# One masked product per head in a state-space chunk stage, with two products moved to GpSimd

## The reference

```
acs    = cumsum(dt * A)                      # in a chunk
Lmat   = exp(where(i >= j, acs[i] - acs[j], -inf))
y_diag = sum_j (C[i] . B[j]) * Lmat[i, j] * dt[j] * x[j]
y_off  = (C[i] . h_prev) * exp(acs[i])
y      = forward(y_diag + y_off) + backward(y_diag + y_off) + d_skip * x
y      = y * silu(z);  y = y * rsqrt(mean(y * y) + eps) * norm_g
```

## Time and profile before

| | |
|---|---|
| median of 3 runs | 1816.97 us (1810.83 to 1821.08) |
| span of the profiled execution | 1810.1 us (its own time, from the first to the last instruction; the page gives no other) |
| busy in the span | PE 1716.3 (95%), PEld 1410.0, DVE 900.0, ACT 596.6, POOL 402.3 us |
| the chunk stage in it | from about 852 to 1012 us |

### The profile page before, as it was taken

The page is one execution under the profiler, slowest core; times in us unless marked ns, Lnnn a source line. Parts: engine busy times, 40 slices in busy tenths (PEclk is TensorE's granted clock), DMA queues, the critical chain, the costliest instruction groups (busy, mean ns, idle before and its releaser), DMA issues. The chain is left out here.

```text
span 1810.1 us, 27115 instructions
## 1 busy us (share of the span) xinstructions
PE 1716.3 (95%) x10438; PEld 1410.0 (78%) x10439; DVE 900.0 (50%) x1031; ACT 596.6 (33%) x1011; POOL 402.3 (22%) x275
## 2 busy tenths in 40 slices
PE   7999999999999989999999999997999998997997
PEld 6878888877877767777888888786777777785786
DVE  5202777202134137742788424323767789951674
ACT  5211222231111136642455313212543443443232
POOL 1011111111211101002100022000255565652330
PEclk9999999999999989999899999999999999998999
DMA  6211222323456312017675334223856778743452
GB/s 214 79 59 60 79 78 79 120 75 108 131 180 192 109 55 65 27 67 223 203 203 150 123 134 163 68 88 117 307 210 243 269 275 306 287 172 138 132 196 93
DMA packets 115837, 265.91 MB, mean 147 GB/s; under 512 B 13011, under 2 KB 59555, under 8 KB 115740
## 3 DMA queue, kind: packets, MB, share of 16 engines
q1 hardware_dynamic: 99772, 209.76, 35.4%
q0 software_dynamic: 8320, 30.43, 5.0%
q10 hardware_dynamic: 7648, 24.35, 3.8%
HBM read 192.95 MB, written 71.55 MB: 146 GB/s over the span
## 5 line engine op out<-in xcount | busy, mean ns | idle before, releaser
L2187 DVE TENSOR_TENSOR ex_wlo<-ex_raw,ex_whi 128x1024 fp32r<-128x1024 f32 x102 | 152.9, 1501 | 8.5 <-ACT ex_whi L2181 5.2
L2183 DVE CAST ex_whi<-ex_raw 128x1024 fp32r<-128x1024 f32 x96 | 114.3, 1191 | 45.4 <-DMA ex_raw<-experts 40.7
L2765 PE MATMUL rt_p<-ex_whi,ex_xh 128*128 x280 | 114.5, 409 | 14.5 <-DVE ex_wlo L2187 8.6
L286 PE MATMUL rest_p<-hi_h,whi_in 128*128 128x512 f32 (+1 forms) x480 | 122.2, 363 | 0.0
L286 PE MATMUL rest_p<-lo_h,whi_in 128*128 128x512 f32 (+1 forms) x480 | 120.5, 359 | 0.0
L286 PE MATMUL rest_p<-hi_h,wlo_in 128*128 128x512 f32 (+1 forms) x480 | 120.1, 359 | 0.0
L2766 PE MATMUL rt_p<-ex_wlo,ex_xh 128*128 x280 | 110.5, 395 | 0.0
L2767 PE MATMUL rt_p<-ex_whi,ex_xl 128*128 x280 | 110.3, 394 | 0.0
L286 PEld LDWEIGHTS rest_p<-hi_h,whi_in 128*128 128x128 f32 x480 | 80.4, 189 | 22.6 <-issue 8.4
L960 POOL TENSOR_TENSOR wlo_in<-wraw_in,whi_in 128x1024 fp32r<-128x1024 f32 x18 | 43.9, 2438 | 229.9 <-ACT whi_in L923 229.9
L929 ACT ACTIVATE rest_out<-rest_p 128x1024 f32<-128x1024 f32 x20 | 20.5, 1025 | 217.3 <-PE rest_p L286 213.7
(11 more groups left out here) (412 smaller groups left out, 4037.6 us busy)
## 6 DMA issues: line engine op xcount, KB each, us to landing
ex_raw<-experts SPq DMA_DIRECT2D x96, 512.0 KB, 6.2
wraw_in<-units SPq DMA_DIRECT2D x36, 512.0 KB, 4.3
y_slots<-ex_y ACTq DMA_DIRECT2D x35, 512.0 KB, 4.2
rest<-rest_out SPq DMA_DIRECT2D x20, 640.0 KB, 5.8
scan_e<-erow SPq DMA_DIRECT2D x32, 256.0 KB, 4.3
xtok<-conv_tok SPq DMA_DIRECT2D x10, 640.0 KB, 3.3
z_x<-x SPq DMA_DIRECT2D x10, 512.0 KB, 4.0
ao_gate<-rest SPq DMA_DIRECT2D x8, 640.0 KB, 5.7
```

The source lines that it names most:

```text
L286: mm = pe.matmul(out[:, n, 0:size], w[:, kk, :], h[:, kk, c:c + size], start=(kk == 0 and w is whi and h is hi), stop=(kk == ktiles - 1 an ...
L2183: eng.tensor_copy(self.hi[:, e % 2, n, :], self.raw[e % 2][:, n, :]).then_inc(self.w_hi[n], 1)
L2187: eng.tensor_tensor(self.lo[:, e % 2, n, :], self.raw[e % 2][:, n, :], self.hi[:, e % 2, n, :].bitcast(F32), ALU.subtract).then_inc(self.w ...
L2765: pe.matmul(gu[s][:, :], xh[s][:, kk, :], hi, start=(kk == 0), stop=False)
```

## The change

The exponents of the two directions are no longer closed by matmuls. Both are computed everywhere; then VectorE overwrites, in PSUM, the forward exponents with the backward ones under the mask of the upper or lower triangle (`merge`, a copy under a predicate, two of 512 elements a unit). There is one exponential and one weighing for each pair of merged banks, two of each a unit, and one decay product per head (8 matmuls in place of 16). The diagonal then holds the forward term only; the backward term of the same token, dt times C.B of that token, is added to d_skip. So the skip matrix differs from chunk to chunk: GpSimd makes it for each unit (`diagonal`, 1024 elements, two buffers), after it has worked out the per-token terms once (`same_token`: a product over 1280 elements, six halving sums, two small instructions). For that, C and B of all tokens are loaded once, 1.3 MB, ahead of the first chunk. GpSimd also takes over `carried_c`, 1024 elements a unit. The splitting of the next stage's weights is spread over units 9, 11, 13 and 15. `mx` has four tiles in place of eight.

```
-                for r in range(4):
-                    pe.matmul(seg[:, r, :], idr[:, :], shut[...].to_broadcast([P, 4, P]), start=True, stop=False)
...
+            def carried_c(w):
+                pool.wait_ge(bc_in[s], 64 * (t // 2 + 1))      # g == 0
+                pool.wait_ge(e_in[g], e_loads(t))
+                pool.wait_ge(di_ready, w + 1)
+                pool.tensor_tensor(cs[g][part(t), :, :], es[g][part(t), :, :], cc[s][part(t), g, :]..., ALU.mult)  -> c_ready
+            def diagonal(w):
+                pool.wait_ge(c_ready, w)
+                if w >= 2:
+                    pool.wait_ge(m_used, 4 * w - 7)
+                pool.tensor_tensor(di[g][:, :, :], ident..., per_head(same[:, t, g * HPG:(g + 1) * HPG], P), ALU.mult)  -> di_ready
...
+            same_token()
+            for w in range(UNITS):
+                diagonal(w)
+                carried_c(w)
+                if w in (9, 11, 13, 15):
+                    split_next((w - 9) // 4, w % 4 == 3)
...
 (apply)
+                pe.wait_ge(di_ready, w + 1)
-                        pe.matmul(out[par][:, c, :], x_of(h), di[:, h, :], start=(c == 0), stop=False)
+                        pe.matmul(out[par][:, c, :], x_of(h), di[g][:, h % HPG, :], start=(c == 0), stop=False)
-                    pe.wait_ge(m_ready, 4 * w + c + 1)
-                    for n in range(2):
-                        for par in range(2):
-                            pe.matmul(out[par][:, c, :], x_of(...), mx[(4 * w + c) % 8][:, 2 * par + n, :], ...)
+                    if c == 0:
+                        pe.wait_ge(m_ready, 2 * w + 2)
+                    for par in range(2):
+                        pe.matmul(out[par][:, c, :], x_of(...), mx[(2 * w + par) % 4][:, c, :], ...)
...
+            def exp(w, p):                                     # ScalarE, p = 0, 1
+                act.wait_ge(merged, 2 * w + p + 1)
+                if w == 1:
+                    act.wait_ge(same_step, 9)
...
+            def merge(w, p):                                   # VectorE
+                if p == 0:
+                    dve.wait_ge(seg_done, w + 1)
+                dve.copy_predicated(seg_of(0, p), after, seg_of(1, p)).then_inc(merged, 1)
...
             for w in range(UNITS + 3):                         # VectorE
                 gate(w - 1)
+                merge(w + 1, 0)
+                merge(w + 1, 1)
                 rest(w - 3)
                 weigh(w + 1, 0)
-                weigh(w + 1, 1)
                 norm(w - 2)
-                weigh(w + 1, 2)
-                weigh(w + 1, 3)
-                carried_c(w + 1)
+                weigh(w + 1, 1)
...
+            sp.dma_start(bct..., d["xtok"]...[:, :, D:D + 2 * P]).then_inc(bct_in, 16)   # SP, ahead of chunk 0
```

More of the change, by code:

```diff
@@ L1759, in stage_ssd_scan @@
         cs = [k.at(f"scan_c{s}", [P, HPG, P], F32, O_W + 24576 + 4096 * s) for s in range(2)]
[L1760 to L1762 removed]
+        mx = [k.at(f"scan_m{s}", [P, 4, P], F32, o) for s, o in enumerate((
+            O_W + 32768, O_W + 34816, O_SSD + 2048, O_SSD + 4096))]
+        bct = k.at("scan_bc_tok", [P, NT, 4, SSD_HEAD], F32, O_SSD + 1280)
+        same = k.at("scan_same", [P, NT, N_SSD], F32, O_SSD + 11520)
         es = [tile(f"e{s}", [P, HPG, P]) for s in range(2)]
@@ L1779, in stage_ssd_scan @@
         br = [tile(f"b{s}", [P, KT, P]) for s in range(2)]
-        di = tile("di", [P, N_SSD, P])
+        di = [tile(f"di{s}", [P, HPG, P]) for s in range(2)]
         cb_s = [tile(f"cb{s}", [P, P]) for s in range(2)]
@@ L1878, in _, with same_token @@
             pool.memset(eps[:, :], EPS).then_inc(eps_set, 1)
[L1879 to L1882, removed]
-            for n in range(2):
[L1884 to L1887, removed]
+            def same_token():
+                dt_b = k.ssd.dt[:, :, N_SSD:2 * N_SSD].rearrange("p t (g h) -> p t g h", g=2)
+                out = same[:, :, :].rearrange("p t (g h) -> p t g h", g=2)
+                pool.wait_ge(bct_in, 16)
+                pool.tensor_tensor(bct[:, :, 0:2, :], bct[:, :, 0:2, :], bct[:, :, 2:4, :], ALU.mult).then_inc(same_step, 1)
+                pool.wait_ge(same_step, 1)
+                half = SSD_HEAD
+                while half > 1:
+                    half //= 2
+                    pool.tensor_tensor(bct[:, :, 0:2, 0:half], bct[:, :, 0:2, 0:half], bct[:, :, 0:2, half:2 * half], ALU.add
+                                       ).then_inc(same_step, 1)
+                    pool.wait_ge(same_step, 7 - half.bit_length() + 1)
+                pool.tensor_tensor(out, dt_b, bct[:, :, 0:2, 0:1].to_broadcast([P, NT, 2, HPG]), ALU.mult).then_inc(same_step, 1)
+                pool.wait_ge(same_step, 8)
+                pool.wait_ge(par_in, 32)
+                pool.tensor_tensor(same[:, :, :], same[:, :, :], dsk[:, :].unsqueeze(1).to_broadcast([P, NT, N_SSD]), ALU.add
+                                   ).then_inc(same_step, 1)
+                pool.wait_ge(same_step, 9)
@@ new lines, in diagonal, with split_next @@
+            def diagonal(w):
+                t, g = w // 2, w % 2
+                pool.wait_ge(c_ready, w)
+                if w >= 2:
+                    pool.wait_ge(m_used, 4 * w - 7)
+                pool.tensor_tensor(di[g][:, :, :], ident.unsqueeze(1).to_broadcast([P, HPG, P]),
+                                   per_head(same[:, t, g * HPG:(g + 1) * HPG], P), ALU.mult).then_inc(di_ready, 1)
+            def split_next(n, low):
+                if not low:
+                    pool.wait_ge(next_in, 32)
+                    pool.tensor_copy(next_hi[:, n, :], next_raw[:, n, :]).then_inc(next_split, 1)
+                else:
+                    pool.wait_ge(next_split, 2 * n + 1)
+                    pool.tensor_tensor(next_lo[:, n, :], next_raw[:, n, :], next_hi[:, n, :].bitcast(F32), ALU.subtract
+                                       ).then_inc(next_split, 1)
@@ L1897, in sums @@
                 if w:
-                    pe.wait_ge(exped, 4 * w)
-                for r in range(4):
-                    pe.matmul(seg[:, r, :], idr[:, :], shut[:, r % 2, :].unsqueeze(1).to_broadcast([P, 4, P]), start=True, stop=False)
+                    pe.wait_ge(exped, 2 * w)
                 for c in range(4):
@@ L1942, in apply @@
                 for c in range(4):
-                    pe.wait_ge(m_ready, 4 * w + c + 1)
-                    for n in range(2):
-                        for par in range(2):
-                            mm = pe.matmul(out[par][:, c, :], x_of(2 * (4 * g + c) + par), mx[(4 * w + c) % 8][:, 2 * par + n, :],
-                                           start=False, stop=(c == 3 and n == 1))
+                    if c == 0:
+                        pe.wait_ge(m_ready, 2 * w + 2)
+                    for par in range(2):
+                        mm = pe.matmul(out[par][:, c, :], x_of(2 * (4 * g + c) + par), mx[(2 * w + par) % 4][:, c, :],
+                                       start=False, stop=(c == 3))
                     mm.then_inc(m_used, 1)
@@ L2011, in cb_copy @@
                 if w >= 2:
-                    act.wait_ge(m_ready, 4 * w - 4)
+                    act.wait_ge(m_ready, 2 * w - 2)
                 act.activation(cb_s[w % 2][:, :], cm[:, 0:P], ACT.Copy).then_inc(cb_ready, 1)
[L2016 to L2019, removed]
+            cb_copy(0)
+            exp(0, 0)
+            exp(0, 1)
             for w in range(UNITS + 2):
[L2021 to L2027, removed]
+                if 1 <= w <= UNITS:
+                    square(w - 1)
+                if w + 1 < UNITS:
+                    cb_copy(w + 1)
+                    exp(w + 1, 0)
+                    exp(w + 1, 1)
                 if 1 <= w <= UNITS:
@@ L2087, in _ @@
             dve.wait_ge(par_in, 32)
-            for c in range(4):
-                weigh(0, c)
-            carried_c(0)
+            merge(0, 0)
+            merge(0, 1)
+            weigh(0, 0)
+            weigh(0, 1)
             for w in range(UNITS + 3):
```

51 lines of the change are left out of this document (22 added, 29 removed).

## The result

The changed kernel takes 1829.2 us (median of 4 runs, 1822.8 to 1834.3) against 1815.7 before (1810.8 to 1821.1): a ratio of 1.0083, 95% interval 1.0057 to 1.0109. It is slower by 13.5 us; the forecast was 13.7.

A forecast was written before the change was run, and what follows sets the result against it. TensorE bounded the kernel; afterwards GpSimd's products blocking VectorE would set 8.0 us a unit. 136.0 + 6.8 - 127.1 - 2 = +13.7 us on 1817.0 gave 1830.7, said as 1830; 8-in-10 range 1796 to 1856.

The forecast's parts named there:

- The bound: TensorE in the chunk stage sets the pace at 7.19 us a unit; the change leaves it 5.16 us of work.
- The merge: VectorE's predicated copy in PSUM, two a unit, taken at 0.60 us each; covered by GpSimd's first product.
- The products: GpSimd's two new products in each unit: skip matrix 1.9 us, C times the decays 2.4 us.
- The exclusion: VectorE instructions with two SBUF inputs and GpSimd's SBUF reads exclude one another: 2.85 us a unit against both products.
- The period: One unit of the stage: GpSimd's start delay, two products and VectorE's excluded work, 7.8 us against 7.19 before.
- The clock: TensorE's waiting lowers its granted clock; charged to half of the units, 0.2 us, making 8.0 us a unit.
- rival 3: TensorE's clock stays low, its work about 10 us at half speed for half the time: +29 us, 1846; chance 22%.
- The edges: Outside the steady units: splitting the next weights adds 6.8 us, the stage's start gains 2 (bounds -5 and +5).
- The split: GpSimd's two casts and two subtractions for the next weights, behind the products and exposed: 6.8 us (bounds 0 and 6.8).
- the prediction's own sign: In TensorE's trace of the chunk stage, mean squares 7.5 to 8.4 us apart would confirm the sum.
- The first (products beside VectorE): GpSimd's products exclude nothing or are short: 6.0 us a unit, -27 us, 1790; chance 10%.
- the second: Cheaper GpSimd products, 1.9 us each: 7.3 us a unit, split half hidden, clock kept, -2 us, 1815; chance 20%.

The follow-up runs named there:

- B: The changed kernel with the weighings reading CB from PSUM, ScalarE's copy gone and CB made behind `apply`: 1827.7 us, ratio 1.0072 to the kernel before.
- E: The changed kernel with both GpSimd products, C times the decays and the skip matrix, moved to VectorE: 1807.9 us, ratio 0.9966 to the kernel before.
- A: The changed kernel with the skip product done twice in each unit, giving TensorE 0.92 us more work: 1817.8 us, ratio 1.0026 to the kernel before.
- G: D plus weighings reading CB from PSUM, both ahead of rest: 1816.5 us, ratio 1.0006 to the kernel before.
- D: The changed kernel with C times the decays moved to VectorE, skip matrices left on GpSimd: 1803.7 us, ratio 0.9954 to the kernel before.
- H: G with SP issuing x and the states ahead of the repeated decays, and C times the decays ahead of rest: 1812.6 us, ratio 1.0010.

## Why the prediction was right, and where its parts were not

**The bound.** TensorE's work was put at 5.16 us a unit. At half clock and busy throughout, a unit takes 10.46, twice 5.23: right.

**The merge.** 0.60 us taken; two take 1.27 as recorded, the same as two weighings in the earlier trace rows, and they run beside GpSimd's product. Right, and its cover held.

**The products.** 1.9 and 2.4 us; measured 1.90 and, where nothing held it back, 2.34. Right: the product with one value repeated was cheaper than that with a repeated row.

**The exclusion.** Right, shown by B from one side (an operand moved to PSUM frees the weighing) and by E from the other (without the products the weighings keep 0.69 us). The trace of the change agrees with the Trainium skill (SBUF — State Buffer, section Who interferes with whom) in both halves: merge and gate at 0.70 us at most, weighings up to 2.84.

**The period.** 0.65 + 1.9 + 2.4 + 2.85 = 7.8 us. Measured from product to product, 924.92 to 932.52, it is 7.6, and the mean squares stand 7.51 apart. The start after the last weighing was 0.74 for 0.65; most of the rest of the difference is rest, which slips in between the two products and costs them some 0.4 us in place of 0.6. But this period ruled only four of the seventeen units outright, and TensorE waited for the weighing in seven units only, not in each (877 to 1010 us; total us, times, longest):

```profile
PE scan_y L1996 <- DVE scan_m L2094: 15.0, 7, 3.8
```

The first four units took 24.3 us in place of 31.2. In the first two VectorE had fewer norms and rests to do (they begin at 880.9 and 886.0); in the fourth, of 5.55 us, C times the decays came 2.76 us late for want of its loads, beside gate and merges, and held neither weighing nor norm.

**The clock.** This is the term that was mis-sized. "I charge it to half of the units: 0.2", 3.4 us in all. Six units ran at TensorE's half speed; at 7.5 each they would have taken 45.0 us, they took 61.6, so it cost 16.6 in this execution. The mechanism named for rival 3 (TensorE's work becomes about 10 us at half speed) was right for these six, a third of the stage and not the half that the rival took. What I missed is that the slack of 2.6 us, set against that rival, is of no use once the clock stays low: 10.3 us of work leave no slack, TensorE is the bound itself, and from 975 on the clock stayed down though TensorE no longer waited. The slack does cover a short fall. In the unit of 7.51 us from 925.59, two groups were slowed (1.76 and 1.93 us in place of 1.09 and 1.04), and VectorE still set the pace:

```profile
929.90 1.93 PE L1990 MATMUL scan_y<-scan_c,scan_h 128*64 128x128 f32 x16
```

Which wait brings the clock down is not settled. This fall came behind a wait of 1.01 us (924.33); in B TensorE waited 1.25 us or more in each unit from 900 to 925 at a clock of 1.00.

**The edges.** The split cost 4.3 us for 6.8: two units with a subtraction, 9.67 and 9.59, against 7.5; the units with a cast cost nothing. But each subtraction made TensorE wait 3.5 us or more, and a half-speed stretch followed both. The start gained 0.3 us for 2, comparing one execution of each kernel.

So 136.0 + 6.8 = 142.8 us was forecast for the seventeen units and 142.6 came. That they agree to 0.2 us, and the medians' difference to the same 0.2, is luck: the prediction named the right parts, and their errors, of both signs, cancelled: the clock 13 us more than charged, the first units 7 less, the split 2.5 less, the four steady units 2.6 less, the rest 1 less. By the prediction's own sign, mean squares 7.5 to 8.4 us apart, the sum is not confirmed: the mean is 8.4, but only two units (7.51 and 7.52) lie in that range. The profiled execution was also the longest of four, so the stage of a median run was probably shorter. The carried C's wait for its loads, which I named as something that would make me wrong, did come, 5.4 us in five waits, but the unit of 8.9 that it lengthened follows the one of 5.55 that it shortened.

**Rivals.** The first (products beside VectorE) fell by B and E; the second by the prices. The third was true of a third of the units, and A, in whose trace the slow row at the end is gone, gives back 11 us.

## What to carry to other kernels

Before work moves to GpSimd, count on VectorE the instructions with two SBUF inputs: in this kernel the move added GpSimd's time to theirs, and 1.2 us of VectorE became 2.3 us of exclusion. Putting one operand in PSUM freed the weighing, but what produces it then lay on the path. And when TensorE's work a unit is cut below the pace of another engine, price its waiting at both clock levels: a lighter TensorE at half speed was slower here than a heavier one at full speed.

## What the chip showed that was not expected

- The lower clock level can hold while TensorE is busy throughout. In B it was granted 0.50 from 975 to 1000 with 25.00 of 25 us busy. Rows of more than two long units are in the change, in B and in G; the four versions with the skip product twice have none, but neither have D, E and H. What lets the clock rise in one case and not in the other the runs don't show.
- Small instructions are held one by one. In the changed kernel the four of a norm, 1.13 us in the earlier trace rows, took 5.72 beside three GpSimd instructions:

```profile
917.95 5.72 DVE L2113 SCALAR_TENSOR_TENSOR scan_v<-scan_u,scan_gain,scan_rs 128x128 f32<-128x128 f32 x4
917.96 1.90 POOL L1925 TENSOR_TENSOR scan_di<-const,scan_same 128x1024 f32<-128x1024 f32 x1 [4.53 <-PE scan_y L1996]
...
920.00 2.48 POOL L1915 TENSOR_TENSOR scan_c<-scan_e,scan_cc 128x1024 f32<-128x1024 f32 x1
...
922.43 1.10 POOL L1931 CAST whi_so<-wraw_so 128x1024 fp32r<-128x1024 f32 x1
```
